# Low halves of weights moved from GpSimd to VectorE in part of a six-block kernel

## The reference, cut to what matters

```
x = x + conformer_conv_mixer(rms(x))      # phase 0: 31-tap depthwise convolution
x = x + forgetting_attention_mixer(rms(x))# phase 1: 16 heads of 128, q and k normalised per head
x = x + short_conv_mixer(rms(x))          # phase 2: 3-tap convolution
x = x + conformer_conv_mixer(rms(x))      # phase 3
x = x + mixers(rms(x)) @ w_out            # phase 4: three attentions, gated and summed
x = x + (silu(gate) * up) @ w_ffn_out     # phase 5: feed forward
```

## Time and profile before

| what | value |
|---|---|
| median of 3 runs | 1706.01 us (1705.09 to 1707.49) |
| the profiled execution | 1704.73 us, span of the trace 1702.9 us |
| PE busy | 1593.6 us, 94% of the span |
| DVE busy | 934.9 us, 55% |
| ACT busy | 855.7 us, 50% |
| POOL busy | 741.6 us, 44% |
| low halves on POOL | 210, 481.7 us |
| low halves on DVE | 179, 254.6 us |

### The profile page before, as it was taken

One profiled execution on the slowest core, in us unless ns is written; L12 is line 12 of the kernel. 1 busy time (PEld: TensorE's weight loads), 2 busy tenths in 40 slices (PEclk: granted clock), 3 DMA queues, 4 the chain that ended last, 5 costly groups with the idle time before them and its releaser, 6 DMA issues.

```text
span 1702.9 us, 28287 instructions
## 1 busy us (share of the span) xinstructions
PE 1593.6 (94%) x10947; PEld 1454.9 (85%) x10947; DVE 934.9 (55%) x2023; ACT 855.7 (50%) x1526; POOL 741.6 (44%) x572
## 2 busy tenths in 40 slices
PE   4999878999999989999899988899999999889998
PEld 3888778998788989999888878898887778889998
DVE  3799965444565554444379998423035545633332
ACT  2577764553455444444357776443325646444442
POOL 0688853332222424444258895365411112334432
PEclk8999989999999999999999999999999999999999
DMA  4654435446553546766444434675752112646654
GB/s 127 143 146 135 130 108 175 133 165 127 122 123 124 163 135 177 195 175 197 124 124 137 136 128 138 152 186 140 182 153 71 51 56 86 194 136 177 187 156 125
DMA packets 341453, 240.11 MB, mean 141 GB/s; under 512 B 36925, under 2 KB 328475, under 8 KB 341320
## 3 DMA queue, kind: packets, MB, share of 16 engines
q1 hardware_dynamic: 329880, 231.33, 47.7%
q10 hardware_dynamic: 10992, 6.29, 1.7%
q0 software_dynamic: 448, 0.69, 0.5%
HBM read 236.55 MB, written 1.74 MB: 140 GB/s over the span
## 4 chain that ended last, share of the span: by engine, by line
PE 70%; DVE 17%; ACT 5%; issue 4%; POOL 2%; DMA 1%; SPq 1%; DVEq 0%; POOLq 0%; ACTq 0%
PE bank L598 8%; DVE bank L876 8%; PE bank L599 8%; PE bank L600 8%; PE bank L634 4%; PE bank L636 4%; PE bank L635 4%; PE bank L990 4%; PE bank L1288 3%; PE bank L596 3%; PE bank L1289 3%; PE bank L1290 3%; PE bank L610 2%; DVE wlo L371 2%; PE bank L1083 1%
## 5 line engine op out<-in xcount | busy, mean ns | idle before, releaser
L371 POOL TENSOR_TENSOR wlo<-ring,whi 128x1024 fp32r<-128x1024 f32 (+3 forms) x210 | 481.7, 2295 | 786.0 <-ACT whi L362 785.9
L362 ACT CAST whi<-ring 128x1024 fp32r<-128x1024 f32 (+4 forms) x389 | 379.2, 990 | 274.8 <-PE bank L600 106.2
L598 PE MATMUL bank<-xh,whi 128*128 128x256 f32 x1384 | 402.4, 291 | 32.4 <-DVE xl L562 19.4
L371 DVE TENSOR_TENSOR wlo<-ring,whi 128x1024 fp32r<-128x1024 f32 (+3 forms) x179 | 254.6, 1423 | 267.0 <-ACT whi L362 266.1
L599 PE MATMUL bank<-xl,whi 128*128 128x256 f32 x1384 | 397.0, 287 | 0.0
L600 PE MATMUL bank<-xh,wlo 128*128 128x256 f32 x1384 | 396.7, 287 | 0.0
L598 PEld LDWEIGHTS bank<-xh,whi 128*128 128x128 f32 x1384 | 271.2, 196 | 42.3 <-issue 39.8
L599 PEld LDWEIGHTS bank<-xl,whi 128*128 128x128 f32 x1384 | 271.6, 196 | 0.2
L600 PEld LDWEIGHTS bank<-xh,wlo 128*128 128x128 f32 x1384 | 271.2, 196 | 0.0
L819 POOL TENSOR_TENSOR scratch<-scratch 128x256 f32<-128x256 f32 x288 | 211.3, 766 | 127.0 <-ACT scratch L764 123.1
L596 PE MATMUL bank<-sqb,ring 128*128 128x256 f32 x1024 | 230.1, 385 | 17.3 <-DVE xl L562 9.7
(11 more groups left out here) (254 smaller groups left out, 2640.5 us busy)
## 6 DMA issues: line engine op xcount, KB each, us to landing
ring<-in_a_w_in_dram SPq DMA_DIRECT2D x64, 512.0 KB, 5.2
ring<-in_b_w_in_dram SPq DMA_DIRECT2D x32, 1024.0 KB, 5.8
ring<-in_c_w_in_dram SPq DMA_DIRECT2D x64, 512.0 KB, 5.4
ring<-in_w_in_dram SPq DMA_DIRECT2D x26, 1024.0 KB, 5.4
ring<-in_w_ffn_in_dram SPq DMA_DIRECT2D x44, 512.0 KB, 5.1
ring<-in_a_w_in_dram SPq DMA_DIRECT2D x16, 1024.0 KB, 5.3
ring<-in_a_w_out_dram SPq DMA_DIRECT2D x16, 1024.0 KB, 5.0
ring<-in_w_ffn_out_dram SPq DMA_DIRECT2D x16, 704.0 KB, 4.5
```

The lines of the kernel that those rows point to most:

```text
L362: nc.scalar.copy(piece(whi, h)[:, :, 0:n], src).then_inc(hi_done, 1)
L371: engine.tensor_tensor(piece(wlo, h)[:, :, 0:n], src, piece(whi, h)[:, :, 0:n].bitcast(F32), ALU.subtract).then_inc(done, 1)
L598: nc.tensor.matmul(o, wh[:, k, :], xh[:, k, :], start=(k == 0), stop=False)
```

## The change

A third value of the mark, ALL, gives every low half of a unit to VectorE. It is set for all input projections of phase 1 (attention), phase 2 (short convolution) and phase 5 (feed forward), for all output projections of phases 1, 2 and 4, and in the two long convolutions (phases 0 and 3) for the second half of the output projection's rows (kb = 1). Unchanged are: everything else in the long convolutions, the input, gate and branch projections of the mixers, and the last projection of the feed forward. No wait, no order, no buffer and no ScalarE or TensorE instruction is edited. The core of the diff:

```diff
+        ALL = "all"
@@ cut
-                halves.append((u, ap, k, n, dve and len(halves) % 2 == 0))
+                halves.append((u, ap, k, n, dve == ALL or (dve and len(halves) % 2 == 0)))
@@ plan_out
-        def plan_out(w, nk):
-            return [(kb, g, unit_in(w[kb * D:(kb + 1) * D, :], [(2 * g * P, 2 * P)], True))
+        def plan_out(w, nk, dve="all"):
+            return [(kb, g, unit_in(w[kb * D:(kb + 1) * D, :], [(2 * g * P, 2 * P)], dve if kb == 0 else ALL))
@@ plan_conf
-            n["out"] = plan_out(t["a_w_out"][j], KE)
+            n["out"] = plan_out(t["a_w_out"][j], KE, True)
@@ plan_fox
-            n["f"] = (group((f_e, 1)), unit_in(w, [(4 * E, FH)], True))
-            n["qk"] = [[unit_rows(w, 2 * i, 2, (G % 2) * E + G // 2 * 8 * P, 8 * P, 1) for i in range(4)] for G in range(4)]
+            n["f"] = (group((f_e, 1)), unit_in(w, [(4 * E, FH)], ALL))
+            n["qk"] = [[unit_rows(w, 2 * i, 2, (G % 2) * E + G // 2 * 8 * P, 8 * P, 1, ALL) for i in range(4)] for G in range(4)]
-                n["slots"] += [(kind, i, s, a, unit_rows(w, 4 * a, 4, c0, 4 * P, 2)) for a in range(2)]
+                n["slots"] += [(kind, i, s, a, unit_rows(w, 4 * a, 4, c0, 4 * P, 2, ALL)) for a in range(2)]
@@ plan_short (and the same for "bz", and for "gu" in plan_ffn)
-                n["uc"].append((group((c_cu, c + 1)), unit_in(w, [(c * P, P), (2 * E + c * P, P)], True)))
+                n["uc"].append((group((c_cu, c + 1)), unit_in(w, [(c * P, P), (2 * E + c * P, P)], ALL)))
```

More of the change, by code:

```diff
@@ L273, in unit_block, with unit_rows @@
             return len(units) - 1
-        def unit_rows(w, k0, nk, c0, width, per):
+        def unit_rows(w, k0, nk, c0, width, per, dve=True):
             src = w[k0 * P:(k0 + nk) * P, c0:c0 + width].rearrange("(k p) n -> p k n", p=P)
             units.append((width, [(nk, 0, width, src)]))
-            cut(len(units) - 1, False, True, rows_of=per)
+            cut(len(units) - 1, False, dve, rows_of=per)
             return len(units) - 1
@@ L467, in plan_short @@
             for c in range(KE):
-                n["uc"].append((group((c_cu, c + 1)), unit_in(w, [(c * P, P), (2 * E + c * P, P)], True)))
-                n["bz"].append((group((y_raw, 32 + c + 1)), unit_in(w, [(E + c * P, P), (3 * E + c * P, P)], True)))
+                n["uc"].append((group((c_cu, c + 1)), unit_in(w, [(c * P, P), (2 * E + c * P, P)], ALL)))
+                n["bz"].append((group((y_raw, 32 + c + 1)), unit_in(w, [(E + c * P, P), (3 * E + c * P, P)], ALL)))
             n["out"] = plan_out(t["c_w_out"][0], KE)
@@ L514, in plan_ffn @@
             n = {"ph": ph}
-            n["gu"] = [(group((y_raw, 64 + i + 1)), unit_in(w, [(i * P, P), (FF + i * P, P)], True)) for i in range(KF)]
+            n["gu"] = [(group((y_raw, 64 + i + 1)), unit_in(w, [(i * P, P), (FF + i * P, P)], ALL)) for i in range(KF)]
             n["out"] = plan_out_ffn(ph, t["w_ffn_out_2"][0], KF, KF // 2)
```

## The result

The changed kernel takes 1716.11 us (median of 5 runs, 1713.66 to 1720.58) against 1706.01 us. The ratio is 1.0059 with a 95% interval of 1.0041 to 1.0077. The forecast was 1714.1 us. The profiled execution took 1716.62 us with a span of 1714.8 us. In the traces of the changed kernel every line of `kernel.py` named here stands two lower than before (L1288 is L1290, L1347 is L1349, L1222 is L1224, L1251 is L1253, L371 is L373).

The account below looks back on a forecast made before the run. TensorE bounds the kernel, busy 94% of the span. Stalls 7.0 + clock 1.7 - gain 0.6 = 8.1 us on the profiled 1704.73 gives 1712.8, plus 1.3 for the median: 1714.1 us; eight-in-ten range 1708.5 to 1719.

Parts of the forecast that it names:

- Counts: Whole kernel: 114 low halves move, VectorE gets 140 us more, GpSimd 274 us less; low halves near 96 and 293.
- Unit i = 2: Q and k projection, group 3: low half of k8 ahead of scale(4) and scale(5) makes k5 begin 3.7 us later.
- Unit i = 3: Q and k projection, group 3: low half of k10 ahead of scales and four copies makes them 2.9 us later.
- Group ends: Q and k projection, ends of groups 0, 1 and 2: low half before the copies costs 0.1 us each, 0.3 in all.
- Unit i = 1: Q and k projection, group 3: low half of k6 and two scales end after spread(4) and spread(5) begin; cost 0.1 us.
- Clock: After group 3's two holes: one clock fall taken, 1.7 us of full-speed time lost; bounds 0 and 3.4.
- Gain: End of the mixers: VectorE's addition takes 0.69 us instead of 2.56 without GpSimd's low half; 0.6 us saved net.
- the likeliest case's own range: Whole kernel: all terms at their ends give 4.7 to 11.4 us of loss, that is 1710.7 to 1717.4 us.
- (1) Taken back: Phase 1: TensorE's later slack absorbs the stalls, about no change, 1706.0 us; chance 0.10.
- (2) Faster by fewer collisions: Whole kernel: collisions are common, so moved halves free VectorE's instructions too; 1701 us, chance 0.05.
- (3) The cover of 0.5 us fails: Short convolution and feed forward: late third piece ahead stalls each input unit, 0.3 us each adds 16; 1730 us, chance 0.08.
- The prediction's own sign of being wrong: Holes in group 3: the forecast is wrong if they bring a longer half-clock stretch than 1.7 us lost each.

Follow-up runs that it names:

- e8: Kernel after, with the two units of the first slot shared between VectorE and GpSimd as before, so 112 of 114 halves move: 1705.03 us, ratio 0.9998.
- e10: Kernel after, with 24 unused matmuls put in front of spread(6) and 24 in front of the first slot's wait, to fill the holes: 1715.15 us, ratio 1.0049.
- e1: Kernel after, with only the q and k projection's low halves shared between VectorE and GpSimd as before: 1715.64 us, ratio 1.0057.
- e7: Kernel before, with only the two units of the first slot given to VectorE alone (low halves of k8 and k10): 1714.93 us, ratio 1.0051.
- e2: Kernel before, with only the q and k projection's low halves given to VectorE alone: 1703.80 us, ratio 0.9990.
- e6: e3 with every low half of the short convolution's and feed forward's inputs computed twice on VectorE: 1718.54 us, ratio 1.0078.
- e3: Kernel after, with VectorE's list preparing one piece less ahead beside each q and k unit, all halves still VectorE's: 1705.41 us, ratio 0.9998.
- e4: Kernel after, with one piece less ahead in VectorE's list only at unit 2 of group 3: 1713.61 us, ratio 1.0045.
- e5: Kernel after, with one piece less ahead in VectorE's list only at unit 3 of group 3: 1714.64 us, ratio 1.0052.

## Why the prediction was right, point by point

- **What bounds it.** Right. Taking 276 us from GpSimd gave nothing measurable (e8), as the earlier trace rows said of a TensorE that is busy 116.22 of 117.00 us, and all the time in the other stages.
- **Counts.** 96 and 293 low halves, as computed. The load was overestimated: +95 us, not +140, since instructions of VectorE got quicker: the price of 1.225 us was read from the short convolution, and the attention loop's was 2.57 before. This is off the path, and the sum had no term for it.
- **Unit i = 2.** Predicted 3.7. Measured by k5's start: 404.72 against 400.64, less 0.2 by which the group was late already, is 3.9. The waits were the ones named, 3.23 and 0.29 us before L1349, released by the scales.
- **Unit i = 3.** Predicted 2.9. Measured 3.53 of idle against 0.78 before: 2.8.
- **Group ends.** Mis-sized: predicted 0.1 each, measured 0.5. TensorE's distance to the kernel before was -1.26, -0.77, -0.28 and +0.21 us at the four groups. The rows of VectorE and TensorE at the end of group 0 show a part that I left out, the step from the end of the copy to the first matmul:

```profile
323.97 2.48 DVE L1253 COPY qk<-bank 128x512 f32<-128x512 f32 x4
...
324.80 0.36 PE L1290 MATMUL bank<-xh,whi 128*128 128x256 f32 x1 [0.27 <-DVE qk L1253]
```

  The first copy begins at 323.97 and runs 0.65 us, to 324.6, and TensorE begins 0.2 us later. I had compared the copy's end with the moment when TensorE wants the bank, as if it could begin at once. That is 0.2 of the missing 0.4. Another 0.1 is that the copy ended 0.2 us after this moment and not 0.1: TensorE's last matmul of the group starts at 324.25 and the next would follow 0.12 us later, at 324.4. The last 0.1 is that the second matmul followed the first after 0.19 us and not after 0.12. 3 x 0.5 = 1.5, over the bound of 1.
- **Unit i = 1.** Predicted 0.1. No wait for it shows in TensorE's list: 0.
- **Clock.** Mis-sized: one fall was taken, both came. By the matmuls, k5 to the end of the group took 414.83 - 404.72 = 10.1 us, against 409.25 - 400.64 = 8.6 before: 1.5. With 1.7 for the second, 3.2; e10 gives 3.0. The bound of 3.4 held it, and that the two falls came out at 1.7 us each was not known beforehand: in e1 and e7, whose holes are as long, the first fall lost 3.4 and the second 1.7, which would have been over the bound.
- **Gain.** Predicted 0.6; its mechanism came, its size is not shown. At the end of the mixers the addition takes 0.69 us, as named:

```profile
1476.65 0.69 DVE L1784 TENSOR_TENSOR qk<-qk,wide 128x512 f32<-128x512 f32 x1
```

  and TensorE's waits for what follows (L1673, before L1671) fell from 4.9 to 4.2 us in total: the first from 2.8 to 0.9, while the second grew from 2.1 to 3.2. But in the same trace TensorE also stood 1.3 us just before, for which the profile names no releaser, and that takes the gain back. Without such a wait the place has 4.2 us in e8 and 3.9 in e1; e2 and e7, where nothing is changed at this place (the addition took 2.57 us in e7), have 4.3. So the gain lies between 0 and 0.7 us.
- **The sum.** In phase 1: 1.5 + 3.9 + 1.5 + 2.8 + 1.7 = 11.4, measured 11.3; predicted 8.7. Phase 4 added 2.2 in the profiled executions. I don't count it as a term of the change: with the same code there, the experiments' phase 4 varied from 398.8 to 403.9 us, and 1.7 of the 2.2 is one fall of the clock that lasted longer, at a place that the change leaves as it was. Windows of 1 us at that place lose 0.38 + 0.50 + 0.50 + 0.33 = 1.7 us from 1174 before, and 0.25 + 6 x 0.50 + 0.17 = 3.4 us from 1183 after. (The three traces with phase 4 as before lie at 398.8 to 399.5, the nine with the changed one at 398.8 to 403.9; that the change has no part in this is likely and not shown.) In the medians the loss was 10.1 us where I had 8.1. Two terms were too small by 1.2 and 1.5 us, the gain was too large if anything, and the time fell inside the likeliest case's own range. It is partly luck that it lies so near: the medians differ by 1.8 us less than the profiled executions, and what that is, no trace shows.
- **Which edit causes it.** The text gave the two holes to the third piece ahead and priced them so, which was right. But the amount listed them under "q and k", and I carried that into e1 and e2: the pieces are the first slot's. A forecast for the whole change could not show this error; the experiments did.
- **Rivals.** (1) Taken back: no, e7 alone costs 0.51%. (2) Faster by fewer collisions: the collisions are real, about 45 us of VectorE's time, yet e8, which has that saving without the holes, is at 0.9998. The Trainium skill, SBUF — State Buffer, section "SBUF: two separate sides", describes the mechanism as an exclusive lock; the traces agree, 2.56 against 0.69 us for the same addition, and 2.57 against 1.22 us for a low half of the attention loop. There, before, one of VectorE's began at 455.14, 0.9 us behind one of GpSimd, and ended at 457.72, 1.08 us after GpSimd's end at 456.64. (3) The cover of 0.5 us fails: no. In the kernel after TensorE has no wait for VectorE within the short convolution, and in e6 it has none in the feed forward even with low halves that come 1.2 us later. In e6's short convolution twice the load was felt, as load.

## What to carry to other kernels

Before work is moved to another engine, look up what stands behind it in that engine's ordered list, and what the moved instruction waits for: here 112 of 114 moves cost nothing and two cost 9 us, because a wait for ScalarE came in front of a hand-over to TensorE. The same two moves are free when the instruction stands one place later in the list (e3). And find by which buffer's or unit's mark an instruction is governed, not in which loop it is issued, before you name a part of a change as the cause.

## What the runs showed that I had not expected

- The clock after one and the same hole is not the same in every execution. After the first hole the kernel after lost 1.7 us; e7, with a hole of the same 3.2 us, went to 0.50 from 404 to 410 us and lost 3.4 (so did e1, and e4 after its only hole). The prediction's own sign of being wrong, more than 1.7 us lost for a hole, thus came in three of the five kernels with holes, though not in the one that it was made for:

```profile
402.00:404.00 2.00, 0.40 (x1) 0.28 (x1) 2.00 (x5) 0.00 (x0) 0.00 (x0) 0.91 1.04 165
...
408.00:410.00 2.00, 2.00 (x12) 2.00 (x11) 0.00 (x0) 0.00 (x0) 0.00 (x0) 0.50 0.00 0
410.00:412.00 2.00, 2.00 (x17) 2.00 (x17) 0.24 (x1) 1.05 (x1) 0.00 (x0) 0.89 0.00 0
```

- Yet a fall followed each of the eight unfilled holes of 3.2 to 3.5 us in group 3 (two each in after, e1 and e7, one each in e4 and e5), and lost either 1.7 or 3.4 us; none came behind the 0.8 us hole that the kernel before has there.
- A phase with the same code may differ by 5 us between two profiled executions (phase 4 of e1 and e10: 398.8 and 403.9). A single profile is thus no measure of a term of 1 or 2 us in it; the rows of the place itself are.
